# Loading the modulation slabs, x and the first weights without a wait, the operand made on ScalarE, and a first projection that runs k-tile by k-tile

## What is computed

```python
c_act = silu(c)                                   # 1024 values
mod = c_act @ w_ada + b_ada                       # 1024 x 6144, split in six
sh1, sc1, g1, sh2, sc2, g2 = split(mod, 6)
h = x * (1.0 + sc1) + sh1                         # the operand "om"
proj = h @ w_in                                   # the first 512 columns are q: "in_q"
q, k, v, qi, ki, wi, gate_b, gate_c, hc = split(proj)
```

## Time and profile before

| | us |
|---|---|
| median of three runs | 1224.65 (1218.98 to 1226.74) |
| the profiled execution | 1227.48 |
| its span | 1225.7 |
| PE busy | 1112.6 (91% of the span) |
| DVE busy | 760.3 (62%) |
| ACT busy | 574.1 (47%) |
| POOL busy | 266.9 (22%) |

### The profile page before, as it was taken

The page is one execution under the profiler, slowest core; times in us unless marked ns, Lnnn a source line. Parts: engine busy times, 40 slices in busy tenths (PEclk is TensorE's granted clock), DMA queues, the critical chain, the costliest instruction groups (busy, mean ns, idle before and its releaser), DMA issues.

```text
span 1225.7 us, 20953 instructions
## 1 busy us (share of the span) xinstructions
PE 1112.6 (91%) x8197; PEld 1024.2 (84%) x8197; DVE 760.3 (62%) x1172; ACT 574.1 (47%) x963; POOL 266.9 (22%) x257
## 2 busy tenths in 40 slices
PE   1999648999999999998999999998998799999998
PEld 1887534879999987887899999998875599999997
DVE  5747876665664446675576555567676676555554
ACT  0545334464454336542455444465455655544452
POOL 0434232013332002011123322013120023332001
PEclk9998855999999999999899999998998999999999
DMA  8654454616554625350155645563433046653650
GB/s 314 214 207 159 184 193 150 205 38 218 167 176 147 186 73 206 138 180 27 46 172 196 205 151 154 176 224 123 150 127 135 1 138 206 205 184 109 199 195 36
DMA packets 188325, 193.46 MB, mean 158 GB/s; under 512 B 13721, under 2 KB 150722, under 8 KB 188130
## 3 DMA queue, kind: packets, MB, share of 16 engines
q1 hardware_dynamic: 184016, 179.88, 43.9%
q0 software_dynamic: 2640, 10.49, 2.3%
q10 hardware_dynamic: 1602, 2.18, 0.5%
HBM read 191.48 MB, written 1.05 MB: 157 GB/s over the span
## 4 chain that ended last, share of the span: by engine, by line
PE 67%; DVE 18%; ACT 5%; DMA 4%; issue 4%; POOL 2%; ACTq 1%; POOLq 0%; SPq 0%; DVEq 0%
PE gemm L1701 20%; PE gemm L1703 19%; PE gemm L1702 19%; DVE wlo L1152 4%; DVE macc L1205 2%; DMA raw<-in_w_in 2%; ACT whi L816 2%; PE aux L2028 1%; POOL om L616 1%; DVE olo L1174 1%; PE aux L1808 1%; DVE xlo L1174 1%; DMA early<-in_w_ada 1%; DMA raw<-in_w_ada 1%; DVE om L1423 1%
## 5 line engine op out<-in xcount | busy, mean ns | idle before, releaser
L1152 DVE TENSOR_TENSOR wlo<-raw,whi 128x1024 fp32r<-128x1024 f32 (+2 forms) x348 | 399.4, 1194 | 111.8 <-ACT whi L816 111.4
L1701 PE MATMUL gemm<-ohi,whi 128*128 128x256 f32 x1536 | 437.8, 285 | 18.0 <-DVE wlo L1152 11.1
L1703 PE MATMUL gemm<-ohi,wlo 128*128 128x256 f32 x1536 | 432.6, 282 | 0.0
L1702 PE MATMUL gemm<-olo,whi 128*128 128x256 f32 x1536 | 431.8, 281 | 0.0
L816 ACT ACTIVATE whi<-raw 128x1024 fp32r<-128x1024 f32 (+2 forms) x348 | 309.3, 955 | 121.8 <-PE gemm L1703 95.5
L1701 PEld LDWEIGHTS gemm<-ohi,whi 128*128 128x128 f32 x1536 | 292.4, 190 | 28.6 <-DVE wlo L1152 15.2
L1702 PEld LDWEIGHTS gemm<-olo,whi 128*128 128x128 f32 x1536 | 292.6, 190 | 0.2
L1703 PEld LDWEIGHTS gemm<-ohi,wlo 128*128 128x128 f32 x1536 | 292.3, 190 | 0.0
L1701 PE MATMUL gemm<-acthi,whi 128*128 128x256 f32 x528 | 147.8, 280 | 0.0
L1703 PE MATMUL gemm<-acthi,wlo 128*128 128x256 f32 x528 | 147.3, 279 | 0.0
L1702 PE MATMUL gemm<-actlo,whi 128*128 128x256 f32 x528 | 147.2, 279 | 0.0
(11 more groups left out here) (310 smaller groups left out, 1529.7 us busy)
## 6 DMA issues: line engine op xcount, KB each, us to landing
raw<-in_ffn_w_in SPq DMA_DIRECT2D x44, 1024.0 KB, 6.1
raw<-in_ffn_w_out SPq DMA_DIRECT2D x32, 704.0 KB, 5.1
raw<-in_gla_w_in SPq DMA_DIRECT2D x6, 2048.0 KB, 7.6
raw<-in_diff_w_in SPq DMA_DIRECT2D x6, 2048.0 KB, 7.7
raw<-in_w_gate SPq DMA_DIRECT2D x11, 1024.0 KB, 5.2
raw<-in_w_up SPq DMA_DIRECT2D x11, 1024.0 KB, 7.5
raw<-in_w_down SPq DMA_DIRECT2D x16, 704.0 KB, 5.1
raw<-in_w_ada SPq DMA_DIRECT2D x5, 2048.0 KB, 8.1
```

The source lines that it names most:

```text
L1152: dve.tensor_tensor(wlo[hslot][:, q * w:(q + 1) * w], raw[slot][:, q * w:(q + 1) * w], whi[hslot][:, q * w:(q + 1) * w].bitcast(F32), ALU. ...
L1701: pe.matmul(dst, st_hi, mv_hi, start=start, stop=False)
L1702: pe.matmul(dst, st_hi, mv_lo, start=False, stop=False)
L1703: return pe.matmul(dst, st_lo, mv_hi, start=False, stop=stop_)
```

## The change

SP no longer waits for the small loads before ada2. POOL no longer makes `om`; ACT makes it, each tile right behind its `ohi`. DVE used to make all four low quarters of in_q and then the eight `olo`; it now makes a quarter before every second `olo`. `keep_warm` before the projection goes from 13 matmuls to 6. The first projection is a function of its own: the loop over the k-tiles is the outer one, and each k-tile is used for all four output tiles, in four PSUM banks at once; it waits for a low quarter every second k-tile. The numbers of matmuls, splits, copies and loads stay.

```diff
--- before.py
+++ after.py
@@ -562,8 +562,6 @@
                     continue
                 if not ph.ring:
                     i = int(ph.name[3:]) - 2
-                    if i == 0:
-                        sp.wait_ge(params_in, 16 * (len(ROWS_A) + len(ROWS_B) + 4))
                     for dst, src in sources[ph.name](0, early[i]):
                         sp.dma_start(dst, src).then_inc(early_in[i], 16)
                     if i == 1:
@@ -610,11 +608,6 @@
                     me.did(pool.tensor_tensor(tl(rope_out, 7), tl(rope_in, 7), C("cos_i", T), ALU.mult), rope_cos)
 
 
-            pool.wait_ge(res_in, 4)
-            pool.wait_ge(mod_set, 1)
-            for t in range(KT):
-                me.did(pool.tensor_scalar(tl(om, t), tl(res, t), mod[:, 8 + t:9 + t], mod[:, t:t + 1],
-                                          ALU.mult, ALU.add), om_ready)
             rope_cosines(0)
             rope_cosines(1)
             POOL_ROPES = {4: (2, 3)}
@@ -887,7 +880,8 @@
             for t in range(KT):
                 me.did(act.activation(tl(ohi, t), tl(res, t), ACT.Identity, bias=mod[:, t:t + 1],
                                       scale=mod[:, 8 + t:9 + t]), ohi_ready)
-                me.seen(om_ready)
+                me.did(act.activation(tl(om, t), tl(res, t), ACT.Identity, bias=mod[:, t:t + 1],
+                                      scale=mod[:, 8 + t:9 + t]), om_ready)
 
             def evac(dst_of, sem_, scale_of=None):
                 def one(ph, at, t):
@@ -1223,12 +1217,11 @@
             me.again(dve_read)
             me.link(dve.tensor_tensor(mod[:, 0:16], X[3][:, 0:16], A("b_ada", 0, 16), ALU.add), mod_read)
             me.did(dve.tensor_scalar(mod[:, 8:16], mod[:, 8:16], 1.0, None, ALU.add), mod_set)
-            for q in range(4):
-                low(PH["in_q"], At(0), q)
             for t in range(KT):
-
-                dve.wait_ge(om_ready, t + 1)
-                me.seen(om_ready)
+                if t % 2 == 0:
+                    low(PH["in_q"], At(0), t // 2)
+
+                me.next(om_ready)
                 me.next(ohi_ready)
                 me.did(dve.tensor_tensor(tl(olo, t), tl(om, t), tl(ohi, t).bitcast(F32), ALU.subtract), olo_ready)
             me.did(dve.tensor_scalar(res[:, :], res[:, :], ALPHA, None, ALU.mult))
@@ -1772,6 +1765,22 @@
                     banks.skip(G[0], freed, base + ph.n)
                     banks.skip(G[1], freed, base + ph.n)
 
+            def first_projection():
+
+                ph = PH["in_q"]
+                hi, lo = (slab_view(ph, b[ph.j0 % 2], "plain") for b in (whi, wlo))
+                for k in range(KT):
+                    if k % 2 == 0:
+                        pe.wait_ge(lo_ready, 4 * ph.j0 + k // 2 + 1)
+                    pe.wait_ge(olo_ready, k + 1)
+                    for t in range(ph.tiles):
+                        if k == 0:
+                            banks.claim(G[t], rope_src)
+                        ins = three(G[t][:, 0:T], hi[:, k, t * P:(t + 1) * P], lo[:, k, t * P:(t + 1) * P],
+                                    tl(ohi, k), tl(olo, k), k == 0, k == KT - 1)
+                        if k == KT - 1:
+                            ins.then_inc(tile_done, 1)
+
             def stats(tok=False):
 
 
@@ -1830,10 +1839,10 @@
                                            tl(xin, tt, w=D)[:, (2 * n + k) * P:(2 * n + k + 1) * P], ident)
                 ins.then_inc(setup_t, 1)
             modulation(3)
-            keep_warm(G[2], 13, ones[:, :])
+            keep_warm(G[2], 6, ones[:, :])
 
             banks.claim(X[3], mod_read)
-            gemm("in_q", rope_src, olo_from=0)
+            first_projection()
 
             pe.wait_ge(const_in, 16)
             pe.wait_ge(p_in, 16)
```

## The result

| | before | after |
|---|---|---|
| median of the runs | 1224.89 us (1218.98 to 1228.31, 12 runs) | 1228.49 us (1226.18 to 1232.89, 12 runs) |
| profiled execution | 1227.48 us | 1232.89 us |
| in_q, first and last start of a matmul | 43.49 and 57.87 | 41.85 and 54.56 |
| in_idx, first and last start | 58.79 and 69.95 | 60.87 and 74.55 |
| load of in_gc begins | 68.44 | 73.01 |

The ratio after to before is 1.0039, interval 1.0021 to 1.0058: the changed kernel is slower by 3.6 us between the medians and by 4.8 us by the ratio, well inside 1%. The first projection does end 3.3 us sooner, as its order promised. The second starts 2.1 us later and takes 2.5 us longer, and the load behind it is 4.6 us late.

The account below looks back on a forecast made before the run. TensorE was taken as the bound of the whole kernel. In_idx's start (-0.2 us) and its clock (+1.5) summed to +1.3: 1226.0 us against the median 1224.65, range 1218.5 to 1231.0, "same" at 0.95.

Parts of the forecast that it names:

- the sum: In_idx's start -0.2 us plus its clock +1.5 us: +1.3 us on the whole kernel; chance 0.58.
- in_idx's clock: In_idx starts at half clock after a 5 us pause: +1.5 us, up to 3.0, 0 if it escapes.
- The parts' upper bound: +5.1 us in all: 3.0 cold in in_q, 2.0 on the low quarters, 3.0 in in_idx.
- The landing of the slabs: All slabs land 2.0 to 2.5 us sooner, taken as 2.3, with 0.7 us lost to the small loads.
- my limit of 19.4: Biases are needed on PE by about 19.4 us; each us beyond costs one.
- Rival 2: Small loads kept waiting, ada2 starts later: 1230.0 or 1236.3 us; chance 0.10 inside 1%, 0.02 beyond.
- The removed wait: DVE's 1.96 us of idle time before ada2 goes; `mod_set` moves to 36.33, -1.95 us.
- ScalarE's pairs: `ohi` and `om` at 0.50 us each, one k-tile per 1.0 us, last at 46.6; PE begins at 40.1.
- in_q by itself: Last start 51.3 at full clock, -6.6 us; 2.0 us lost to a cold clock makes it 53.3.
- The quarters behind tile 0's copy: In_idx's quarters 1 to 3 wait for the copy at 52.5; lows lose 1.0 us; in_idx starts at 58.6.
- Rival 1: Clock stays up in in_q and in_idx, POOL meets no low quarter: in_idx at 55.6, -3.2, 1221.5 us; chance 0.26.
- Rival 3: In_idx's slab still lands at 50.5, changing nothing: 1226 us; part of the forecast's 0.58.

Follow-up runs that it names:

- experiment 9: Changed kernel with six small loads (four lam_in rows, two gates) issued by SyncE behind in_idx's slab: 1227.34 us, ratio 1.0009.
- experiment 3: Changed kernel with SP's wait on the small loads put back before ada2: 1229.08 us, ratio 1.0036.
- experiment 4: Kernel before with only SP's wait on the small loads taken out: 1225.04 us, ratio 0.9991.
- experiment 5: Changed kernel with thirteen warm matmuls instead of six: 1230.42 us, ratio 1.0033.
- experiment 7: Changed kernel with six small loads (four lam_in rows, two gates) issued later by ScalarE, behind the load of p: 1233.61 us, ratio 1.0073.
- experiment 11: Kernel of experiment 1 with `om` made on POOL again: 1222.26 us, ratio 0.9977.
- experiment 8: Changed kernel with in_idx's quarters split before tile 0's copy, thirteen warm matmuls, and six small loads issued later by ScalarE: 1222.47 us, ratio 0.9985.
- experiment 1: Changed kernel with all four quarters of in_idx's slab split before tile 0 of in_q is copied: 1221.74 us, ratio 0.9965.

## Why the prediction was right, and where its steps were off

The forecast was "about the same, +1.3 us"; it came out +3.6 by the medians (+4.8 by the ratio), inside its range, and by the mechanism named: in_q's gain is given back as a pause ahead of in_idx with VectorE's `wlo` as the releaser, and in_idx starts at half clock. By the trace the sum should have been +4.6 (load against load). The three misses that count all went the same way, 1.3 us in in_q's end, 1.0 in the low quarters and 1.0 in in_idx's clock; the width of the range held them, not the sum. The parts' upper bound, too, adds up to +4.8 and not to the +5.1 written there. The terms:

- **The landing of the slabs, 1.5 us of in_q's start, was the wrong step.** I took 2.3 us sooner for all slabs, and 0.7 us as the price of the small loads. in_q's slab landed at 19.19 + 16.99 = 36.18, 0.9 sooner than the earlier trace rows had it; ada2 let VectorE start at 23.23, where I had it landed at 21.7. The DMA rows, queue, number of records, MB and share, first of the changed kernel in 14 to 15, 15 to 16 and 16 to 17 us, and then over 11 to 21:

```profile
q1 hardware_dynamic: 49, 0.08, 36.5%
q10 hardware_dynamic: 48, 0.01, 4.4%
...
q1 hardware_dynamic: 149, 0.29, 77.7%
q10 hardware_dynamic: 151, 0.03, 15.4%
...
q1 hardware_dynamic: 140, 0.29, 83.4%
q10 hardware_dynamic: 140, 0.03, 14.5%
...
q1 hardware_dynamic: 1475, 2.98, 84.0%
q10 hardware_dynamic: 709, 0.21, 8.5%
```

  and of experiment 9 over 11 to 21:

```profile
q1 hardware_dynamic: 1977, 3.98, 104.2%
q10 hardware_dynamic: 89, 0.02, 1.0%
```

  The queues do take turns record by record, 149 to 151 and 140 to 140. In two stretches of 0.1 us, 15.2 to 15.3 and 15.5 to 15.6, each queue moved about one record for each of the 16 engines:

```profile
q1 hardware_dynamic: 16, 0.03, 74.6%
q10 hardware_dynamic: 17, 0.00, 15.0%
...
q1 hardware_dynamic: 17, 0.03, 89.2%
q10 hardware_dynamic: 16, 0.00, 17.8%
```

  The earlier trace rows had shown the same, with the parts exchanged: there the small records are the slab queue's (38 in 0.00 MB) and the large ones ScalarE's, so it was not the full slab queue that I called it. The Trainium skill ("DMA: Bandwidth & Descriptors", section "Queues, rings and completion order") has typically 9 to 17 descriptors in a turn; these rows don't agree with it. But a turn took 16 / 140 = 0.114 us and not 0.087: I had used the pace of slab rows with nearly no small records between them. Of the 568 small records that moved between 14 and 20 us, 48 came in the first, in which both queues nearly stood, 420 in the next three, and 100 in the last two. So PE got its biases at 20.24, 3.0 us behind my 17.2. It was 0.8 us past my limit of 19.4, and still harmless, since ada2 was not there before 23.2 either. And with 620 small records more the slab queue moved 502 rows fewer than in experiment 9, 1.0 MB, or 2.5 us at its 400 GB/s: my 0.7 was too small by more than three times. (163 of the 502 are the gap between this kernel's 49 and experiment 9's 212 in 14 to 15 us, whose cause is open.) The kernel before over the same 11 to 21 us:

```profile
q1 hardware_dynamic: 1263, 2.55, 71.3%
```

  So its dry stretch was worth 1977 - 1263 = 714 rows, 3.6 us where I took 2.7; 2.5 of it went to the small records and 1.1 was left, close to the 0.9 by which in_q's slab came sooner. Rival 2 was thus closer than I gave it.
- **The removed wait** gave 1.0 to 1.2 us at in_idx (experiments 3 and 4). At `mod_set` the trace has 38.11 - 36.62 = 1.5 us, not 1.95, but only 0.8 of it is ada2's (24.04 to 23.23). The other 0.7 is the fourth sum on PE, which took 1.18 us at a higher pace instead of 1.88. `mod_set` no longer decides: `ohi` began 3.3 us behind it, when in_q's slab was split.
- **ScalarE's pairs** came every 0.98 us, as forecast (40.06 to 47.45 for fifteen steps of 0.49), but from 40.06, with the slab. PE started at 41.85, 1.75 late.
- **in_q by itself**: 12.71 us to the last start where 11.2 is full clock, so 1.5 lost to the clock where I took 2.0. Last start 54.56 against 53.3. In the kernel before no slow start of in_q was hidden, as the prediction has it: its first matmuls start at 43.49, 43.68 and 43.80, at full pace, since the thirteen ones had taken the slow stretch.
- **The quarters behind tile 0's copy**: copies at 53.82, 55.05 and 56.26, 1.22 apart, as forecast. From the first copy to in_idx it took 7.05 us and not 6.1: both of POOL's products met a low quarter, so 5.63 us for three where three alone take 3.7. That is 1.9 lost, about the upper bound I gave, where I took 1.0.
- **in_idx's clock**: 13.68 us from first to last start where before it was 11.16, so 2.5 us; I took 1.5, with 3.0 as the bound. 5.3 us at half clock times 45% is 2.4.

In short: -0.2 for in_idx's start became +2.1 (1.3 from in_q's end, 1.0 from the low quarters), and +1.5 became +2.5. Rival 1 fell in all three of its parts. Rival 3 stood half: in_idx's slab came only about 1.5 us sooner (ScalarE's wait for it ended at 49.06 against 50.55, where I took 2.3), and it changed nothing, since the first quarter wasn't the one that was waited for.

What stays open: the hole of 14 to 15 us in both queues, what decides when the clock rises, and why experiment 5's two better microseconds aren't in its time.

## What to carry over

When a loop order makes several tiles end together, look at what other engines used to do between their ends: here the copy of tile 0 stood ahead of three quarters of the next slab on ScalarE, and one line that splits them first had the next load begin 7 us sooner. A faster producer is worth nothing once the new order needs its product slower than the old one made it, and a gain ahead of a pause of 5 us is paid back in the clock as well. Small loads with nothing waiting for them belong behind the big ones, on a queue whose engine has no work of its own.

## What the runs showed that I had not expected

- **Small records cost a slab queue by their number more than by their bytes.** 0.19 MB in some 620 records went with 1.0 MB of slab rows fewer, 0.8 of a row for each record, or 0.55 without the stretch of 14 to 15 us (above).
- **A DMA issue costs its engine.** On ScalarE six took 3.5 us, 0.44 to 0.66 each (experiment 7); it did no activation meanwhile.
- **The same stream of ones and the same projection met different clocks.** Six warm matmuls and then 1.43 or 1.89 us of idle time gave a full-clock in_q (experiments 9 and 11), six and 4.03 us one that fell (after), thirteen and 3.40 us a full-clock one (experiment 8). The moment of the rise also differs where the program does not: up to in_q the changed kernel and experiment 1 are the same, yet the twelve records of ones that took 1.58 us after the change took nearly twice that there:

```profile
36.98 2.91 PE L1808 MATMUL gemm<-ones 128*128 128x128 f32 x12
```

  There in_q came 2.02 us behind the ones and ran at half pace from its start:

```profile
42.00:46.20 4.20, 4.20 (x20) 4.20 (x21) 3.89 (x7) 4.20 (x10) 0.00 (x0) 1.00 1.01 209
46.40:54.90 8.50, 8.50 (x75) 8.50 (x74) 7.80 (x9) 6.13 (x10) 0.00 (x0) 1.00 0.43 80
```

  The clock column says 1.00 in both rows, but 20 matmuls in 4.2 us against 75 in 8.5 is about half the pace. Early in a trace, before the column first changes, read the clock from the matmuls.
- **VectorE and POOL slow each other.** Three low quarters beside 3.83 us of POOL took 5.63 us, four with POOL silent 4.63 (experiment 1). So VectorE lost 1.9 us, half of POOL's time, and POOL's two products took 2.03 and 1.80 us where one with no low quarter beside it took 1.29 (kernel before, at 58.66).
